# Two edits in a two-layer hybrid transformer step: attention steps one further apart, and MoE routing that works out the row indices first

## What is computed

```
h = rms_norm(x, p['norm1']) * (1.0 + scale1) + shift1
proj = h @ p['w_in']                       # q, k, v | chunk MLP | short convolution
s = einsum('bqkgd,bmkd->bkgqm', q, k) * scale          # 8 query heads, 2 key heads, head_dim 64
p = softmax(s);  attn = einsum('bkgqm,bmkd->bqkgd', p, v)
merged = concatenate([rms_norm(attn, on[:512]), rms_norm(sgu, on[512:768]), rms_norm(conv, on[768:])])
x = x + gate1 * (merged @ p['w_out'])
h2 = rms_norm(x, p['norm2']) * (1.0 + scale2) + shift2
# hierarchical MoE: best of 4 groups, then the best 2 of its 4 experts; 16 experts, D_EXPERT 256
g_idx = argmax(g_logits);  p_g = softmax(g_logits)[g_idx]
top_v, top_i = top_k(softmax(e_logits of that group), 2);  weight = p_g * top_v / sum(top_v)
x = x + gate2 * sum over the 2 experts of weight * ((silu(h2 @ w1) * (h2 @ w3)) @ w2)
```

## Time and profile before

| what | value |
|---|---|
| median of 3 executions | 1190.57 us |
| the profiled execution | 1189.58 us, of it span 1187.7 us |
| busy: TensorE / VectorE / ScalarE / GpSimd | 952.4 / 674.0 / 589.1 / 269.1 us |
| mean granted TensorE clock | 0.893 of full speed |
| moved by DMA | 248.34 MB, mean 209 GB/s |
| chain that ended last | TensorE 63%, DMA 11%, VectorE 10%, ScalarE 7%, issue 5% |

### The profile page before, as it was taken

The page is one execution under the profiler, slowest core; times in us unless marked ns, Lnnn a source line. Parts: engine busy times, 40 slices in busy tenths (PEclk is TensorE's granted clock), DMA queues, the critical chain, the costliest instruction groups (busy, mean ns, idle before and its releaser), DMA issues.

```text
span 1187.7 us, 14999 instructions
## 1 busy us (share of the span) xinstructions
PE 952.4 (80%) x5232; PEld 748.1 (63%) x5232; DVE 674.0 (57%) x938; ACT 589.1 (50%) x900; POOL 269.1 (23%) x302
## 2 busy tenths in 40 slices
PE   3799989896997399999149998889699719999920
PEld 0588866664884278887138886566578617888710
DVE  0358134554454589997354922445437367998826
ACT  1653144544322088987276224454433127898722
POOL 2033033111141211220431401421104121122133
PEclk9999989897997599999569999889999659999965
DMA  9954116173228579998643221437224527999843
GB/s 329 273 225 166 54 49 244 60 296 113 96 108 337 192 296 404 417 413 301 235 181 105 74 71 48 176 127 267 101 88 149 159 92 262 396 421 413 326 158 143
DMA packets 85951, 248.34 MB, mean 209 GB/s; under 512 B 25644, under 2 KB 30252, under 8 KB 75656
## 3 DMA queue, kind: packets, MB, share of 16 engines
q1 hardware_dynamic: 72760, 209.54, 47.1%
q0 software_dynamic: 11696, 32.84, 8.0%
q10 hardware_dynamic: 1440, 5.24, 1.1%
HBM read 221.05 MB, written 30.21 MB: 212 GB/s over the span
## 4 chain that ended last, share of the span: by engine, by line
PE 63%; DMA 11%; DVE 10%; ACT 7%; issue 5%; POOL 2%; SPq 0%; POOLq 0%; ACTq 0%; DVEq 0%
PE ps L1324 12%; PE ps L1326 11%; PE ps L1325 11%; DMA pool<-in_moe_w 5%; PE ps L1331 4%; PE ps L1333 3%; PE ps L1332 3%; PE ps L1341 3%; PE ps L1463 3%; PE ps L1474 2%; DMA raw<-in_w_ada 2%; PE ps L1523 2%; PE ps L1448 2%; PE ps L1590 2%; ACT wH L829 2%
## 5 line engine op out<-in xcount | busy, mean ns | idle before, releaser
L1324 PE MATMUL ps<-wH,actH 128*128 128x512 f32 x608 | 248.3, 408 | 14.0 <-DVE actL L1272 12.5
L1326 PE MATMUL ps<-wH,actL 128*128 128x512 f32 x608 | 241.0, 396 | 0.0
L1325 PE MATMUL ps<-wL,actH 128*128 128x512 f32 x608 | 240.4, 395 | 0.0
L1192 DVE TENSOR_TENSOR wL<-raw,wH 128x2048 fp32r<-128x2048 f32 x64 | 146.1, 2285 | 12.2 <-ACT wH L829 11.7
L1324 PEld LDWEIGHTS ps<-wH,actH 128*128 128x128 f32 x608 | 116.9, 192 | 38.5 <-issue 13.8
L1326 PEld LDWEIGHTS ps<-wH,actL 128*128 128x128 f32 x608 | 116.4, 191 | 26.0
L1325 PEld LDWEIGHTS ps<-wL,actH 128*128 128x128 f32 x608 | 117.2, 193 | 22.8
L829 ACT ACTIVATE wH<-raw 128x2048 fp32r<-128x2048 f32 x64 | 122.1, 1911 | 5.7 <-DMA raw<-in_moe_w 5.7
L1331 PE MATMUL ps<-wH,actH 128*128 128x512 f32 x256 | 105.4, 412 | 4.6 <-DVE wL L1192 3.3
L1333 PE MATMUL ps<-wH,actL 128*128 128x512 f32 x256 | 102.4, 400 | 0.0
L568 POOL DMA_INDIRECT pool<-h2s,idxc x32 | 56.9, 1777 | 200.5 <-PE ps L1590 182.2
(11 more groups left out here) (221 smaller groups left out, 1612.5 us busy)
## 6 DMA issues: line engine op xcount, KB each, us to landing
raw<-in_w_ada SPq DMA_DIRECT2D x48, 1024.0 KB, 7.2
raw<-in_moe_w SPq DMA_DIRECT2D x96, 512.0 KB, 7.2
raw<-in_w_in SPq DMA_DIRECT2D x16, 1024.0 KB, 9.1
raw<-in_moe_w SPq DMA_DIRECT2D x16, 1024.0 KB
pool<-in_moe_w SPq DMA_DIRECT2D x32, 512.0 KB
pool<-in_moe_w SPq DMA_DIRECT2D x16, 1024.0 KB
ys<-pool SPq DMA_DIRECT2D x32, 512.0 KB, 11.8
raw<-in_w_out SPq DMA_DIRECT2D x8, 1024.0 KB, 7.9
```

Source lines behind the costliest of these rows:

```text
L1192: dve.tensor_tensor(wL[:, i, :], mraw[parity][i], f32(wH[:, i, :]), ALU.subtract).then_inc(sem(f"m_lo{i}"), 1)
L1324: pe.matmul(out, aH, wH[:, slot_, cols_], start=first, stop=False)
L1325: pe.matmul(out, aH, wL[:, slot_, cols_], start=False, stop=False)
L1326: return pe.matmul(out, aL, wH[:, slot_, cols_], start=False, stop=last)
```

## The change

**Attention.** The transposes of a step's probabilities now stand two steps behind its scores on TensorE (before: one), and what follows them moves by a step; the loop has 44 steps' worth of turns instead of 43. On ScalarE the copy to `pT` now falls in even turns, ahead of that turn's exponential; on VectorE in odd turns. The statistics of a tile are taken in two parts: the chunk MLP and convolution branches early (`rest_squares`, `rest_stats`, `normalise_rest`), the attention branch when it is done (`attn_square`, `attn_stats`, `normalise_attn`).

**Between projection and routing.** `normalised(2)` moves ahead of `second_half(3)`, the stores of h2 are issued earlier, `h2_chunks(3)` moves ahead of `router(2)`, and the eight `ada_next` units, which stood between these, now stand four ahead of the count matmuls and four between them and the list matmuls.

**Routing.** Ranks by comparison of all pairs take the place of maxima and equality; the counts are read from PSUM; the table of equalities `one_r` compares bfloat16 with bfloat16; row indices come before the block table; the softmax parts, the slots and gates come behind them; the first two gathers take their indices from `idxs` itself, the memset of a gather buffer is gone, and VectorE waits for these gathers to be issued (`first_gathers`) before it splits weights. ScalarE copies the first weights' high parts ahead of the two exponentials. `modc_cols` and `modc_out` move into and behind the block loop.

```diff
@@ gpsimd
-                def branch_stats(t):
-                    pl.wait_ge(sem("ss3"), at("ss3", l, 3 * t + 3))
+                def attn_stats(t):
+                    pl.wait_ge(sem("ss3a"), at("ss3a", l, t + 1))
...
+                def rest_stats(t):
+                    pl.wait_ge(sem("ss3b"), at("ss3b", l, 2 * t + 2))
...
                 bias_in(l, 1)
+                rest_stats(0)
+                attn_stats(0)
                 piece_out(l, 1)
                 bias_in(l, 2)
-                branch_stats(0)
-                branch_stats(1)
-                branch_stats(2)
+                rest_stats(1)
+                attn_stats(1)
+                rest_stats(2)
+                attn_stats(2)
                 piece_out(l, 2)
...
-                pl.wait_ge(sem("list_psum"), at("list_psum", l, 1))
-                pl.memset(xg[:, 1, :], 0.0).then_inc(sem("xg_zero"), 1)
...
+                pl.wait_ge(sem("idx_ready"), at("idx_ready", l, 1))
+                for parity in range(2):
+                    gather(parity, idxs)
+                    pl.sem_inc(sem("m_idx"), 1)
+                pl.sem_inc(sem("first_gathers"), 1)
+                pl.wait_ge(sem("ctl_ready"), at("ctl_ready", l, 1))
                 h = pl.value_load(ctl[0:1, 0:1], min_val=MINB // 2 - 2, max_val=MAXB // 2 - 2) + 1
-                for parity in range(2):
-                    take_idx(parity, parity)
-                    gather(parity)
@@ vector, attention
-                    if u % 2 == 0 and 2 <= u <= NT * NH:
-                        w = u - 1
+                    if u % 2 and 3 <= u < NT * NH + 2:
+                        w = u - 2
...
-                    if u % 2 == 0 and u >= 4:
-                        pair_out(u // 2 - 2)
+                    if u % 2 and u >= 5:
+                        pair_out((u - 5) // 2)
                     if u in W_AT:
                         split_lo(W_AT[u])
                     if u >= 16 and u % 8 == 0:
-                        normalise(u // 8 - 2)
+                        normalise_rest(u // 8 - 2)
+                        normalise_attn(u // 8 - 2)
+                    if u == NT * NH:
+                        normalise_rest(NT - 1)
@@ vector, routing
+                def ranks(v):
+                    link(dve.tensor_tensor(diff, v.unsqueeze(2).to_broadcast([P, NT, 4, 4]), bc(v, 4), ALU.subtract))
+                    link(dve.tensor_tensor(diff, diff, mid(eps_, NT), ALU.is_gt))
+                    link(dve.reduce_sum(rank, diff, X))
...
+                link(dve.tensor_tensor(one_r, bc(qb, P), mid(iota[:, :], 10), ALU.is_equal))
...
+                link(dve.tensor_copy(pr2[:, 0:LB], ps[:, 0, 0:LB]))
+                dve.scalar_tensor_tensor(out=idxs[:, :], in0=pr2[:, 0:LB], scalar=float(NOROW - 1), in1=ps[:, 0, LB:2 * LB],
+                                         op0=ALU.add, op1=ALU.add).then_inc(sem("idx_ready"), 1)
...
+                dve.wait_ge(sem("first_gathers"), at("first_gathers", l, 1))
                 m_split(0, 0, first)
+                if l + 1 < DEPTH:
+                    piece_add(l + 1, 0)
                 m_split(1, 0, first)
@@ tensor, attention
-                    if 1 <= u <= NT * NH:
-                        w = u - 1
+                    if 2 <= u < NT * NH + 2:
+                        w = u - 2
@@ tensor, router
-                ada_next(0, 3)
+                router(1)
+                h2_chunks(2)
+                h2_chunks(3)
                 router(2)
-                h2_chunks(3)
-                ada_next(3, 5)
+                h2_chunks(4)
                 router(3)
-                h2_chunks(4)
-                ada_next(5, 6)
                 router(4)
-                ada_next(6, KD)
+                ada_next(0, 4)
...
+                ada_next(4, KD)
                 pe.wait_ge(sem("lists"), at("lists", l, 1))
```

More of the change, by code:

```diff
@@ L528, in _ @@
                     pl.dma_start(arow[:, c, :], row(modrow[l][c, 4 * D:5 * D])).then_inc(sem("scale2_row"), 16)
-                for t in range(3, NT):
-                    branch_stats(t)
+                rest_stats(3)
+                rest_stats(4)
+                attn_stats(3)
+                attn_stats(4)
                 pl.dma_start(n2row, row(I["norm2"][l])).then_inc(sem("norm2_row"), 16)
@@ L742, in _ @@
                 q_hi(1)
-                for u in range(NT * NH + 3):
-                    if u % 2 and u < NT * NH:
-                        w = u - 1
+                for u in range(NT * NH + 4):
+                    if u % 2 == 0 and 2 <= u < NT * NH + 2:
+                        w = u - 2
                         keys = 5 * P if w >= NH else P
@@ L832, in _ @@
                 w_read(act, l, 11)
+                m_split(0, 0, pairs)
+                m_split(1, 0, pairs)
                 for i in range(2):
@@ L1179, in _ @@
+                for c in range(2):
                     link(dve.tensor_tensor(M[:, c].rearrange("p t (g e) -> p t g e", g=4), bc(og, 4),
-                                           o.unsqueeze(2).to_broadcast([P, NT, 4, 4]), ALU.mult))
-                dve.tensor_tensor(Mb, M[:, 0], M[:, 1], ALU.add).then_inc(sem("choice"), 1)
-                if l + 1 < DEPTH:
-                    piece_add(l + 1, 0)
+                                           o12[:, :, c, :].unsqueeze(2).to_broadcast([P, NT, 4, 4]), ALU.mult))
@@ new lines, in _ @@
+                link(dve.tensor_reduce(em1, es, X, ALU.max))
+                link(dve.scalar_tensor_tensor(out=e2, in0=o12[:, :, 0, :], scalar=-1e30, in1=es, op0=ALU.mult, op1=ALU.add))
+                link(dve.tensor_reduce(em2, e2, X, ALU.max))
+                dve.tensor_tensor(d_, em2, em1, ALU.subtract).then_inc(sem("rt_exp_in"), 1)
+                link(dve.tensor_tensor(eb, eb, own, ALU.add))
+                link(dve.tensor_tensor(own, own, over[:, :, 0], ALU.mult))
+                link(dve.tensor_tensor(eb, eb, own, ALU.subtract))
@@ L1631, in _ @@
                 x_chunks(1, first + 1, 1, pairs)
+                if l + 1 < DEPTH:
+                    modc_cols(l + 1)
                 with pe.Fori(0, h) as pair:
```

259 lines of the change are left out of this document (134 added, 125 removed).

## The result

The changed kernel took 1143.03 us (median of 4 executions, 1140.82 to 1145.23) against 1190.43 for the kernel before (4 executions, 1189.55 to 1191.44): a ratio of 0.9602, 95% interval 0.9579 to 0.9624. It is 47.4 us faster where 29.8 were forecast. The direction and the places were right; the size was too small by more than the range allowed for.

The account below looks back on a forecast made before the run. TensorE held 63% of the chain, but links change by stage: an attention hole, then nearly one chain from h2 to the first low part. Attention 11.4, layer 1 12.0, layer 0 6.4: 29.8 us less, median 1161, range 1150 to 1173.

Parts of the forecast that it names:

- the hole: Attention: VectorE stands still 3.84 us for GpSimd's first-tile roots; closing it makes steps 18 to 20 gain 5.9 a layer.
- rival with a loss: Slower than forecast: layer 0's lists 1167 (0.15), attention's end 1166 (0.12), ScalarE loop 1238 (0.02), block loop paced by transfers 1179 (0.05).
- So the extra step hides the 0.52 wait only to the next limit: 0.1 for each of some five pairs: Attention pairs without modulation: 4.68 us now, limited to 4.58 after; gain called 0.6 us a layer.
- Pairs with modulation units are full of TensorE work, nothing there: Attention pairs with modulation units: no gain from the extra step.
- the loop of 4.58 through VectorE: Attention: scores, maximum, copy, transposes, values, next scores; claimed to limit a pair without modulation after the change, against 4.68 now.
- The end as a whole: End of attention: longer drain, less what the last tile's shorter statistics give back; 0.8 us a layer lost.
- 5.9 + 1.9 = 7.8 us a layer: Attention without the extra step: 5.9 at steps 18 to 20, and the last tile's tail shrinking from 4.39 to 2.5.
- 0.6 - 2.7: Attention, extra step alone: 0.6 us a layer gained in pairs, 2.7 lost as the last head moves from +19.0 to +21.7.
- if steps two apart took over 5 us: Attention, a sign of being wrong: 4.5 to 4.7 us were expected between the scores two steps apart.
- nothing in the change makes it earlier: it follows the output projection: Between attention and router: h2's last tile, ready at 932.87 in layer 1, gains nothing.
- 9.15 us: Router: one transpose group and two routers left after h2's last tile, at low clock; layer 1 gains 3.2.
- rival 3: Clock stays up, no gap between router tiles: 4.5 less in layer 1, 4 in layer 0, perhaps 1 in attention; 1152; chance 0.11.

Follow-up runs that it names:

- two runs with early squares: Rest-branch squares moved from steps 36 and 37 to 29 and 30: in the changed kernel, 1143.46 us; with transposes back to one step behind the scores, 1148.60 us.
- one step behind with early squares: Changed kernel with transposes and what follows back to one step behind the scores, and squares moved from steps 36 and 37 to 29 and 30: 1148.60 us.
- the run with late gates: Changed kernel with eleven small slot and gate instructions and the register load moved between the halves of the first low part: 1141.62 us, ratio 0.9584.

## Why the prediction fell short

**The bound and the places** were read rightly: the hole, the router's order, the routing chain and the gathers gave the gain, and the block loop kept its length. No rival with a loss came true.

**The step that failed most** is "So the extra step hides the 0.52 wait only to the next limit: 0.1 for each of some five pairs" with "Pairs with modulation units are full of TensorE work, nothing there". I charged the extra step at the end (2.7; measured 3.1, since step 36 to the last division takes 22.1 instead of 19.0) and did not credit it at the start. A pipeline that is one step deeper defers a step's transposes and values: the steps 10 to 12 took 6.99 us instead of 8.67, with the values (1.31) moved behind them, and the first sixteen steps 2.5 less. Drain and start belong together, and I counted one of them. The pairs gave more too, 1.1 from step 20 to 36 and 0.3 from 16 to 18: the loop of 4.58 through VectorE holds for a steady pair (4.56), but the first pair behind a tile with modulation takes 4.00. With steps 18 to 20 at 6.3 less instead of 5.9 a layer comes to 9.3: -2.5 - 0.3 - 6.3 - 1.1 + 0.9. The end as a whole, with 2.2 given back behind the last division, came out as forecast (0.9 for 0.8).

The two runs with early squares part this more sharply. The one with one step behind has everything of attention's change but the extra step, for which the forecast was 5.9 + 1.9 = 7.8 us a layer; against the kernel before it has 7.6 and 8.4. For the extra step alone the forecast was 0.6 - 2.7, a loss of 2.1; those two runs have a gain of 1.7 and 1.2. So the excess in attention lies in this one term, and part of what steps 18 to 20 gave is the extra step's: without it they take 4.89, with it 4.11, of which the next pair gives 0.7 back (5.35 for 4.68). That pair is also the one sign of being wrong that came true, "if steps two apart took over 5 us"; what holds TensorE in it is not shown.

**From attention to h2.** "nothing in the change makes it earlier: it follows the output projection" was wrong: 1.05 a layer came back with the order alone; the changed kernel has 1.4 and 1.3 from attention's end to that tile, and the other 0.3 is not assigned. Before, the last tile of h2 was scaled right behind tile 3, which was late itself; now tile 3 is done 7.7 us ahead of it (3.0 before).

**Router.** 9.15 us were forecast for one transpose group and two routers at the low clock; at the low clock they take 8.71. The size missed is the clock, 1.9 in layer 1: rival 3, to some two fifths of the 4.5 that I had given it there. (Two small slips in my sum there: 932.87 + 9.15 is 942.02, a gain of 3.35, and half of 9.15 would gain 7.9.)

**Routing in layer 1** held term by term: logits to counts -2.5 (forecast 2.4), counts to lists -1.2 (1.1), lists to indices -2.5 (2.4). `one_r` takes 1.49 us with both inputs in bfloat16, as taken; the Trainium skill (Vector Engine (DVE) Microarchitecture Reference, section 5.1) had it so for a repeated element, and the trace agrees. Indices to low part: -3.5 (2.9); it was VectorE that was late, as said, and the run with late gates shows it.

**Layer 0.** The four loads took 14.0 us from the first issue (362.04 to 376.0), 13 forecast. The lists waited as forecast; what was missed ahead of them is again h2 and the clock. Indices to low part gave 2.6 against 1.3: the gathered rows came 8.7 us behind the indices, not late enough to matter as much as I had allowed.

**The sum.** Attention 7.3 more than forecast, h2's tile 2.7, the router 4.8, indices to low part 1.9, less 0.5 for logits to indices: 16.2. Take off the 1.6 elsewhere, and add 3.0, because of the profiled executions one lies above its median and one below: 17.6. The range was made of rivals that were each one mechanism; that the unpriced terms all leaned one way was not in it.

## What to carry to other kernels

When a software pipeline gets one step deeper, write down the start and the drain together: the work that is paid at the end was deferred at the start, and only their difference is a cost. Its value depends on what else stands on the engines: here it gave 1.2 to 1.7 us a layer, and it made room for work on ScalarE that cost 7 to 10 us without it. Before moving a wait's cause behind the waiting instruction, ask which buffers its matmuls free: the lists got 4.7 us earlier and the block 3 us later.

## What was not expected of the hardware

The same 40 TensorE matmuls (transposes and 20-column products) took 5.87, 6.85 or 8.71 us in layer 1, by when the granted clock fell from full to half (2.4 to 1.2 GHz). TensorE was busy 97 to 98% of these stretches; what it had done before the fall were the last 512-column matmuls of the projection and then only transposes and 20-column products. I had expected a fall behind gaps alone. This may be part of why executions of one kernel differ: the five of one step behind with early squares spread over 7.0 us (1144.94 to 1151.90).
